# Moving the first weight loads to another DMA queue and building the warm-up constants on another engine

## The reference

```
hn   = RMSNorm_pre(x)
proj = hn @ W_in            -> [q | k | v | gate_a | u_pool | gate_b]
y_a  = StickBreakingAttn(q, k, v) * silu(gate_a)     (8 heads x 128)
y_b  = MultiScalePool(u_pool) * silu(gate_b)         (4 groups x 256)
x    = x + RMSNorm_post(concat(y_a, y_b) @ W_out)
```

## Time and profile before

| | |
|---|---|
| median of 3 runs | 720.27 us (720.0 to 722.43) |
| profiled execution, its own time | 720.85 us |
| its span, first to last instruction | 719.1 us |
| PE busy | 708.2 us (98% of the span) |
| DVE / ACT / POOL busy | 584.6 / 434.6 / 72.1 us |

### The profile page before, as it was taken

The page is one execution under the profiler, slowest core; times in us unless marked ns, Lnnn a source line. Parts: engine busy times, 40 slices in busy tenths (PEclk is TensorE's granted clock), DMA queues, the critical chain, the costliest instruction groups (busy, mean ns, idle before and its releaser), DMA issues.

```text
span 719.1 us, 9876 instructions
## 1 busy us (share of the span) xinstructions
PE 708.2 (98%) x3740; PEld 610.7 (85%) x3740; DVE 584.6 (81%) x750; ACT 434.6 (60%) x577; POOL 72.1 (10%) x93
## 2 busy tenths in 40 slices
PE   8999999999999999999999999999999999999995
PEld 6878888888888888888888888888888888888884
DVE  3399987988798888888897978898888984376787
ACT  4675476566675656766765676756688434253561
POOL 0000000210020110011110011020001000001001
PEclk9999999999999999999999999999999999999998
DMA  8975446667746667655766665656654307468986
GB/s 284 364 226 135 133 104 167 169 169 198 177 122 170 158 182 174 175 148 148 198 136 177 176 168 159 172 133 173 181 174 176 118 14 250 118 172 227 277 319 234
DMA packets 38831, 128.59 MB, mean 179 GB/s; under 512 B 4352, under 2 KB 5376, under 8 KB 37888
## 3 DMA queue, kind: packets, MB, share of 16 engines
q1 hardware_dynamic: 31728, 102.78, 42.5%
q0 software_dynamic: 6912, 25.17, 20.9%
q10 hardware_dynamic: 144, 0.01, 0.0%
HBM read 123.74 MB, written 4.19 MB: 178 GB/s over the span
## 4 chain that ended last, share of the span: by engine, by line
PE 91%; DMA 3%; DVE 2%; SPq 1%; issue 1%; ACT 1%; POOL 0%; DVEq 0%; POOLq 0%; ACTq 0%
PE ps L1865 36%; PE ps L1870 19%; PE ps L1776 9%; PE ps L1777 9%; PE ps L1775 9%; PE ps L1809 7%; DMA x_rows<-x 3%; PE ps L1898 1%; PE ps L1896 1%; DVE mix L1682 1%; SPq L515 0%; SPq L529 0%; SPq L518 0%; DVE mix L1585 0%; ACT x_hi L638 0%
## 5 line engine op out<-in xcount | busy, mean ns | idle before, releaser
L1865 PE MATMUL ps<-a_ops,w_hi 128*128 128x512 f32 x1120 | 281.4, 393 | 0.0
L1865 PEld LDWEIGHTS ps<-a_ops,w_hi 128*128 128x128 f32 x1120 | 201.8, 189 | 36.8
L1107 DVE TENSOR_TENSOR raw_lo<-raw,w_hi 128x1024 fp32r<-128x1024 f32 x155 | 189.0, 1225 | 22.6 <-ACT w_hi L657 21.6
L657 ACT ACTIVATE w_hi<-raw 128x1024 fp32r<-128x1024 f32 x155 | 163.7, 1056 | 69.1 <-PE ps L1870 60.1
L1870 PEld LDWEIGHTS ps<-a_ops,raw_lo 128*128 128x128 f32 x1120 | 152.8, 190 | 11.0
L1870 PE MATMUL ps<-a_ops,raw_lo 128*128 128x256 f32 x1120 | 156.2, 282 | 0.0
L1730 POOL DMA_DIRECT2D raw<-w_heads x40 | 34.9, 874 | 316.5 <-DMA raw<-w_heads 263.0
L1775 PE MATMUL ps<-w_hi,a_ops 128*128 128x512 f32 x160 | 62.3, 390 | 0.0
L1777 PE MATMUL ps<-w_hi,a_ops 128*128 128x512 f32 x160 | 62.3, 389 | 0.0
L1776 PE MATMUL ps<-raw_lo,a_ops 128*128 128x512 f32 x136 | 53.0, 389 | 0.0
L1556 DVE TENSOR_TENSOR raw_lo<-raw,w_hi 128x1024 fp32r<-128x1024 f32 x23 | 28.2, 1225 | 25.7 <-ACT w_hi L1010 25.7
(11 more groups left out here) (222 smaller groups left out, 1036.6 us busy)
## 6 DMA issues: line engine op xcount, KB each, us to landing
raw<-w_heads SPq DMA_DIRECT2D x100, 512.0 KB, 4.5
raw<-w_heads POOLq DMA_DIRECT2D x40, 512.0 KB, 5.9
raw<-w_out SPq DMA_DIRECT2D x35, 512.0 KB, 4.9
raw<-w_v SPq DMA_DIRECT2D x15, 512.0 KB, 10.1
x_rows<-x SPq DMA_DIRECT2D x6, 1024.0 KB, 12.5
mix<-xT SPq DMA_DIRECT2D x16, 256.0 KB, 9.8
raw_more<-w_out SPq DMA_DIRECT2D x6, 512.0 KB, 6.7
out<-mix SPq DMA_DIRECT2D x6, 512.0 KB, 2.7
```

Of the source, the lines that this page charges most:

```text
L657: act.activation(hi_slot(g), raw_slot(raw, slot), ACT.Copy).then_inc(w_hi_done, 1)
L1107: dve.tensor_tensor(raw_slot(raw_lo, slot), raw_slot(raw, slot), hi_slot(g).bitcast(F32), ALU.subtract).then_inc(w_split, 1)
L1865: pe.matmul(dst, hi[:, k * P:(k + 1) * P], a_ops[:, a:a + SEQ], start=k == 0 and p in (0, 1, 5), stop=False, skip_group_check=True)
```

## The change

It does three things.

First, the two loads of K tile 0's weights are taken out of SP's stream, where they stood between `load_x(0)` and `load_x(1)`, and issued by ScalarE's queue, right behind the load of `pre_gain_col` and ahead of ScalarE's activation table load.

Second, `fill` and `neg_ones` are now written by VectorE as the first thing it does, with semaphores of their own (`filled`, `ones_ready`). GpSimd keeps `positions` and `neg_tri`, the latter behind a wait for `filled`; `POOL_CONSTS` becomes 2.

Third, the matmuls ahead of step 0 are 8 in place of 10, use `neg_ones` as the stationary operand too, and wait for `ones_ready` alone.

```diff
-WARM = 10
+WARM = 8
...
+        filled = sem("filled")
+        ones_ready = sem("ones_ready")
...
-        POOL_CONSTS = 4
+        POOL_CONSTS = 2
...
             load_x(0)
-            for g in range(2):
-                sp.dma_start(raw[:, g * BANK:(g + 1) * BANK],
-                             w_v[g * KK][:, 0:BANK]).then_inc(w0_loaded[g], 16)
             for i in (1, 2):
...
             act.dma_start(pre_gain_col[:, :], pre_gain).then_inc(gain_loaded, 16)
+
+            for g in range(2):
+                act.dma_start(raw[:, g * BANK:(g + 1) * BANK],
+                              w_v[g * KK][:, 0:BANK]).then_inc(w0_loaded[g], 16)
             act.preload_act_table_set("natural_log_exp_and_others")
...
         def _(dve):
+            dve.memset(fill[:, :], -1.0).then_inc(filled, 1)
+            dve.wait_ge(filled, 1)
+            dve.tensor_copy(neg_ones[:, :], fill[:, :]).then_inc(ones_ready, 1)
             dve.memset(neg_half[:, :], -0.5).then_inc(vec_const, 1)
...
-            pool.memset(fill[:, :], -1.0).then_inc(pool_const, 1)
-            pool.wait_ge(pool_const, 2)
-            pool.tensor_copy(neg_ones[:, :], fill[:, :]).then_inc(pool_const, 1)
+            pool.wait_ge(filled, 1)
             pool.affine_select(out=neg_tri[:, :], in_=fill[:, :], compare_op=ALU.is_ge, fill=0.0, base=0,
...
-            pe.wait_ge(pool_const, POOL_CONSTS)
+            pe.wait_ge(ones_ready, 1)
             for _ in range(WARM):
-                pe.matmul(bank(V_BANK[1][TT - 1]).rearrange("p (a b) -> p a b", a=TT), neg_tri[:, :],
+                pe.matmul(bank(V_BANK[1][TT - 1]).rearrange("p (a b) -> p a b", a=TT), neg_ones[:, :],
```

## The result

The changed kernel takes 723.91 us in the median of 14 runs (721.79 to 725.42), the kernel before 720.57 us in 14 runs beside it (720.0 to 722.43). The ratio is 1.0044 with a 95% interval of 1.0036 to 1.0052: 3.3 us slower, where 1.0 us was forecast. It lies above the stated range (719.6 to 723.3) and just inside the band of 0.5%. The runs also scatter more: 3.6 us from lowest to highest, against 2.4 us before.

What follows compares the result with a forecast made beforehand. TensorE's matmul stream, busy 98% of the span, was taken as the bound. Loads +1.0 us, constants and fewer matmuls nothing: 720.27 + 1.0 = 721.3 us, range 719.6 to 723.3.

Steps and rivals of the forecast that it cites:

- the two arms: Before step 6: TensorE's own stream, ready at 39.63, and ScalarE's work behind the last `x_rows` load, meeting at 40.34 us.
- The second arm: Last `x_rows` load to 30.15, then squares, norm, spreading and `w_hi` of step 6; claimed to stay at 40.34 us.
- a rival for that: Before step 6: two queues fill DMA gaps, last `x_rows` load lands 0.5 us earlier; 719.8 us, chance 0.07.
- Part 1: Half-tile loads on ScalarE's queue: second half 1.7 us late by fair turns with SP's queue; +1.0 us (0 to +1.4).
- The gain column's row: At the start: 8 KB on ScalarE's queue landed in 3.0 us, x's first tile in 2.8; taken as sign of turns.
- 0.71 of slack: Before step 6: TensorE's own stream would be ready at 39.63, 0.71 us ahead of 40.34, absorbing that much lateness.
- The table load: ScalarE's activation table load behind two issues would end at 3.4, under the 3.78 of `x_hi`; cost nothing.
- VectorE's constants: Start of the kernel: `neg_ones` ready at 1.09 to 1.46, taken 1.35, so constant matmuls start earlier; gain nothing.
- Part 3: Ahead of step 0: eight constant matmuls in place of ten cost nothing in the likeliest case, covered by the `w_hi` wait.
- The clock rival: Step 0 begins at 1.2 GHz; with loads late +1.0 plus 0.4 to 1.5 us, 721.7 to 722.8; chance 0.18.
- Slower by over 0.5%: Step 0: late loads plus 13 or more slow matmuls at 0.20 us extra; 723.9 us or more, chance 0.04.
- three signs of failure: Half tiles over 2.1 us late, last `x_rows` load moved over 1 us, or over a dozen slow step 0 matmuls.

Runs made afterwards that it cites:

- tile6_before_spreading: The kernel before, with ScalarE's `x_hi` and `w_hi` of tile 6 moved ahead of its eight copies to `rstd_rows`; 720.15 us, ratio 0.9998.
- hold_second_x_tile: The changed kernel, with SP issuing x's second tile and all behind it only once both half tiles have landed; 722.49 us, ratio 1.0030.
- x_tile_on_scalar_queue: The kernel before with VectorE's square, twelve constant matmuls, and x's first tile on ScalarE's queue, half tiles on SP; 723.80 us, ratio 1.0051.
- loads_only: The kernel before with only the two half-tile loads moved to ScalarE's queue, ten constant matmuls kept; 721.46 us, ratio 1.0021.
- vector_square_ten: The changed kernel with ten constant matmuls on VectorE's square and the half-tile loads back on SP; 720.11 us, ratio 0.9999.
- vector_square_twelve: The changed kernel with twelve constant matmuls on VectorE's square and the half-tile loads back on SP; 720.21 us, ratio 1.0000.
- five_constants: The kernel before with five constant matmuls in place of ten; 721.85 us, ratio 1.0021.
- the bridge: The changed kernel with eight more constant matmuls between the first four and the next four of step 0; 723.30 us, ratio 1.0032.
- seventeen_constants: The changed kernel with 17 constant matmuls in place of 8; 721.23 us, ratio 1.0014.
- constants_only: The changed kernel with the half-tile loads back on SP, keeping VectorE's square and eight constant matmuls; 721.22 us, ratio 1.0012.

## Why the prediction was wrong

**The bound and the two arms.** TensorE's stream and its start were the right thing to look at; all of the change lies ahead of step 1. The second arm, ScalarE's at 40.34, was read rightly and generalized wrongly: it decides in two of six profiled executions, and removing it (tile6_before_spreading) brought 0.1 us. Nor did it stay at its place, as the prediction had it ("so the second arm stays at 40.34"): with the half tiles on ScalarE's queue the last `x_rows` load was used at 27.5 to 28.1 us in four of five profiled executions (30.4 in the fifth), against 28.5 to 30.2 with them on SP. More bytes moved early, 272 GB/s in place of 138 from 4 to 6 us; the prediction had only a rival for that.

**Part 1, half tiles late by taking turns.** That the halves come late because SP's stream runs beside them is shown by hold_second_x_tile. That the two queues take even turns is not shown, and x_tile_on_scalar_queue speaks against it. The gain column's row was thin ground for it: 8 KB and 256 KB that both land about 3 us after their issue fit a fixed delay as well. The sizes: forecast 0 to 2.1 us late, taken 1.7; measured 1.0 to 2.6 in five profiled executions, the middle one 1.4. The net cost was forecast at 1.0 (1.7 less 0.71 of slack); alone it measured 1.2 us (loads_only). The number fits partly by luck: a lateness a little too high and a slack that is mostly not there cancel. The first half's 0.8 us was too much: it was used 0.2 and 0.4 us later in the two executions shown, and within 0.1 us of before in the other three.

**The table load and VectorE's constants.** Right. The table load ended at 3.49, under the 3.80 of `x_hi`. The first constant matmul started at 1.39 (forecast 1.35), the fill took 0.17 us and the copy 0.23, and vector_square_ten shows no cost.

**Part 3, eight in place of ten.** This is the step that failed. The prediction said "the removal costs nothing, covered by the wait for `w_hi`" if the clock still rises and stays, and took this as the likeliest case. It costs 1.0 us alone and about 1.5 us with the halves late. In the one execution of before, the clock rose at the eighth matmul; I took that for the moment of the rise, where it is a draw from a distribution. It rose at 5.0 us in that trace, after the tenth constant matmul in vector_square_ten, not before 10 us in five_constants, and near 11 in the bridge's. The clearest pair is the changed kernel and the bridge: both issue the same eight constants from 1.39 on, all of them slow, and then wait; the first is fast at 6.98, the second still slow at 6.65. The last two constant matmuls were no surplus behind the rise but the cover for executions in which it comes later.

**The rivals.** The clock rival had the mechanism and 0.18. Its price beside late loads was 1.4 to 2.9 us over before; the median measured 3.3. "Slower by over 0.5%" named place, mechanism and even the count, 13 slow matmuls, on which it would decide. That is what the profiled execution shows (4.5 us), and it was given 0.04 since "the ten now had seven slow starts before the rise". That counted one way to a slow step 0, a late rise, and not the other, a fall while TensorE waits for a half tile: the wait was in the prediction's own numbers for late halves, and its effect on the clock was not followed through. Seven of the changed kernel's 14 runs have a mean clock of 0.995 or lower (their median is 724.7 us, that of the other seven 723.3). The prediction's three signs of failure all came in the profiled execution: a half tile more than 2.1 us late, the last `x_rows` load moved by over 1 us, and 13 slow matmuls in step 0.

Open: what made ScalarE's queue get less than an even share, when exactly the clock rises or falls, and how the 3.3 us divide between a late rise, a fall ahead of step 0 and a fall between the halves; no run closes only one of the two gaps. The runs bear out that with constant work up to 0.7 us ahead of step 0 or less, no run's clock or time tells of a slow step 0 (seventeen_constants, vector_square_twelve), that with fewer constants more runs do, and that a wait of 2.7 us cost the clock in all five runs.

## What to carry to other kernels

Matmuls that only keep TensorE's clock up are priced by a distribution: one trace in which the clock rises with two to spare doesn't show that two can go. Run such a change many times and look at the highest runs. Count the waits behind them as well: a change that makes a load late can lose a clock that is already up.

The first load on which everything waits belongs at the head of the queue that carries the bulk, ahead of it; on a second queue it competes with bulk that would have stood behind it, though it is issued no later.

Before slack is subtracted from a cost, see whether the span of the profiled execution is typical: here the 0.6 us over the median was about the slack itself.

## What the runs showed of the hardware

The clock column read 1.00 while matmuls started 0.43 us apart, until the clock had first risen: in the traces of before, of the bridge and of five_constants. Only a fall after that shows there (0.79 and 0.50 in the changed kernel). A high mean clock thus doesn't mean that no matmul ran slow: the bridge's profiled execution has 0.997 and a slow start of step 0. constants_only has six runs with 0.998 and spans of 718.9 to 720.0 us, beside its profiled one with 0.998 and 718.4; slow matmuls before the first rise are the likely cause of that spread, which no trace of them shows.

In the profile of five_constants the granted clock read 0.95 from 12 us to the end, the mean of the execution 0.948, with the matmuls keeping their 0.227 us. Its time (721.43 us) is among the lower ones of that kernel. The windows of its profile:

```profile
12.00:16.00 4.00, 4.00 (x20) 3.30 (x19) 3.04 (x8) 1.85 (x2) 0.00 (x0) 0.95 1.03 401
16.00:20.00 4.00, 4.00 (x19) 3.32 (x18) 1.50 (x2) 2.89 (x4) 0.00 (x0) 0.95 1.01 390
```

Two loads of 256 KB issued on a second queue while the bulk queue runs took 5.0 and 7.9 us from issue to landing, and 256 KB of x alone there about 6.4 us (1.24 to 7.70). With only x's first tile beside them, the halves took 4.2 and 4.7 us, and in SP's own queue, in the kernel before, 4.7 and 5.3. The share of busy time hardly tells the cases apart, the bytes do: from 4 to 6 us the DMA engines were busy for 0.86 of the time at 138 GB/s before, and for 0.95 at 272 GB/s in the changed kernel. So the second queue cost these two loads time while more moved in all.
